# Four raw weight buffers and four for high halves, where there were five and three

## The reference, cut to what matters

```python
mod_l = silu(c) @ w_ada + b_ada                 # 6 x 2048 modulation values, and the same from c_ctx
h_l = modulate(rms_norm(x, g), sh_a, sc_a)      # and h_c from ctx
qa, kva, kr, cb, cc, ch = split(h_l @ w_in)     # latent attention (8 heads) and a gated convolution
x = x + gt_a * (mix @ w_out)
x = x + gt_f * (conv_glu(hf @ w_up) @ w_down)   # inner width 5504
x = rms_norm(x, g_final)
# block two, layer A: index scores, top-k, attention of 16 heads, gate, w_o, layer norm, gated embedding
# block two, layer B: stick-breaking attention of 16 heads, gate, w_o, layer norm, gated embedding
```

## Time and profile before

| what | us |
|---|---|
| median of 3 runs (lowest, highest) | 2374.26 (2372.83, 2378.23) |
| the profiled execution: its time | 2373.12 |
| the profiled execution: span from first to last instruction | 2371.4 |
| TensorE, VectorE, ScalarE busy | 2285.2, 1564.9, 1074.3 |
| granted TensorE clock, mean | 0.984 |

### The profile page before, as it was taken

One profiled execution on the slowest core, in us unless ns is written; L12 is line 12 of the kernel. 1 busy time (PEld: TensorE's weight loads), 2 busy tenths in 40 slices (PEclk: granted clock), 3 DMA queues, 4 the chain that ended last, 5 costly groups with the idle time before them and its releaser, 6 DMA issues.

```text
span 2371.4 us, 39488 instructions
## 1 busy us (share of the span) xinstructions
PE 2285.2 (96%) x17584; PEld 2165.7 (91%) x17584; DVE 1564.9 (66%) x1750; ACT 1074.3 (45%) x1014; POOL 42.0 (2%) x80
## 2 busy tenths in 40 slices
PE   6889999998999999999999899999999999999998
PEld 3568878898999999999999899989999999999998
DVE  6777797899868455554556768765567635445674
ACT  6564444334444334443444444445435436664352
POOL 0000000000000000000000000000000000000000
PEclk8999999999999999999999999999999999999999
DMA  8674785696766554455445444333544554335543
GB/s 349 257 275 178 284 302 231 249 350 228 292 249 225 185 189 182 179 185 188 178 181 198 156 179 159 142 120 136 189 160 167 189 179 159 114 135 178 178 160 125
DMA packets 64953, 471.85 MB, mean 199 GB/s; under 512 B 7216, under 2 KB 7216, under 8 KB 8336
## 3 DMA queue, kind: packets, MB, share of 16 engines
q1 hardware_dynamic: 55152, 399.21, 46.4%
q0 software_dynamic: 9488, 68.03, 7.6%
q10 hardware_dynamic: 144, 2.10, 0.2%
HBM read 467.21 MB, written 2.10 MB: 198 GB/s over the span
## 4 chain that ended last, share of the span: by engine, by line
PE 81%; DVE 12%; ACT 3%; issue 2%; DMA 1%; SPq 0%; DVEq 0%; ACTq 0%
PE acc L1898 73%; PE aux L1898 8%; DVE lo L971 4%; ACT hi L404 2%; DVE ada_acc L991 2%; DMA x<-x_t 1%; DVE x L1751 0%; DMA raw<-stream 0%; DVE x L1748 0%; DMA ctx<-ctx_t 0%; DVE rstd L1104 0%; DVE conv_sum L1282 0%; DVE act_lo L1758 0%; DVE rope_scratch L1597 0%; ACT probs L774 0%
## 5 line engine op out<-in xcount | busy, mean ns | idle before, releaser
L971 DVE TENSOR_TENSOR lo<-raw,hi 128x2048 fp32r<-128x2048 f32 x374 | 854.3, 2290 | 641.6 <-ACT hi L404 641.2
L404 ACT ACTIVATE hi<-raw 128x2048 fp32r<-128x2048 f32 x374 | 712.9, 1912 | 817.7 <-PE acc L1898 785.6
L1898 PE MATMUL acc<-act_hi,hi 128*128 128x256 f32 x4464 | 601.4, 288 | 15.1 <-ACT act_hi L730 5.8
L1898 PEld LDWEIGHTS acc<-act_hi,hi 128*128 128x128 f32 x4464 | 566.2, 194 | 30.2 <-issue 19.8
L1898 PE MATMUL acc<-act_lo,hi 128*128 128x256 f32 x4464 | 585.1, 284 | 0.0
L1898 PE MATMUL acc<-act_hi,lo 128*128 128x256 f32 x4464 | 581.2, 283 | 0.0
L1898 PEld LDWEIGHTS acc<-act_lo,hi 128*128 128x128 f32 x4464 | 559.9, 193 | 0.0
L1898 PEld LDWEIGHTS acc<-act_hi,lo 128*128 128x128 f32 x4464 | 555.8, 192 | 0.0
L991 DVE SCALAR_TENSOR_TENSOR ada_acc<-ada_raw,silu_c,ada_acc 128x512 f32<-128x512 f32 x224 | 152.9, 747 | 3.4 <-DMA ada_raw<-ada_stream 2.9
L1898 PE MATMUL acc<-u_hi,hi 128*128 128x256 f32 x688 | 89.8, 283 | 0.0
L1898 PE MATMUL acc<-u_lo,hi 128*128 128x256 f32 x688 | 89.7, 283 | 0.0
(11 more groups left out here) (328 smaller groups left out, 1647.7 us busy)
## 6 DMA issues: line engine op xcount, KB each, us to landing
raw<-stream SPq DMA_DIRECT2D x374, 1024.0 KB, 4.8
ada_raw<-ada_stream POOLq DMA_DIRECT2D x64, 1024.0 KB, 5.9
x<-x_t SPq DMA_DIRECT2D x1, 2048.0 KB, 15.6
ctx<-ctx_t SPq DMA_DIRECT2D x1, 2048.0 KB, 7.8
x<-x_t ACTq DMA_DIRECT2D x1, 2048.0 KB, 8.6
out<-x SPq DMA_DIRECT2D x3, 512.0 KB, 7.2
p_raw<-p_t POOLq DMA_DIRECT2D x1, 512.0 KB, 4.2
out<-x SPq DMA_DIRECT2D x2, 256.0 KB, 2.0
```

Of the source, the lines that this page charges most:

```text
L404: nc.scalar.activation(HI[c % NH][:, :], RAW[c % NR][:, :], ACT.Copy).then_inc(hi_done, 1)
L971: V.tensor_tensor(LO[c % NR][:, :], RAW[c % NR][:, :], HI[c % NH][:, :].bitcast(F32), ALU.subtract)\
L1898: return TE.matmul(out, lhs, rhs, start=start, stop=stop, skip_group_check=True)
```

## The change

Of eight buffers of 8 KB, four instead of five hold raw chunks (and low halves), and four instead of three hold high halves. The modulation groups of the opening lie in the same stream in both kernels. Nothing else changes: the instructions, their order and the addresses behind the eight buffers are the same, but the waits for `pe_chunk` in L349 and L403 have other values, and x % NR and x % NH go through four values.

```diff
-    NR, NH = 5, 3
+    NR, NH = 4, 4
```

## The result

Over 20 runs of each kernel the changed one has a median of 2376.91 us (2374.11 to 2382.78), the one before 2373.41 us (2370.86 to 2378.23): a ratio of 1.0015, 95% interval 1.0008 to 1.0021. The change costs 0.15%, which lies within the 0.2% that the prediction called no change, at its slower end. The profiled execution took 2377.09 us, with a span of 2375.4, 4.0 us longer than before.

A forecast was written before the change was run, and what follows sets the result against it. TensorE, busy 96%, was taken as the bound, with gaps in the opening and around norms and attentions. 2.9 + 3.0 - 0.7 - 0.6 - 1.8 - 1.2 - 2.0 + 1.4 = +1.0 us gave a 2375.3 us median, range 2369.5 to 2381.5.

The forecast's parts named there:

- The rule: Every high half: starts 4.8 us after the end of chunk c-4, not at c-3's end; gain is chunk time minus 4.8.
- Part 1: Opening, context load: issued at 36.45 instead of 33.53 because it waits for chunk 5; +2.9 us, bounds 2.0 to 4.5.
- Part 2: Opening bursts after w_in chunks: later loads, mainly load 38, delay the row copy; +3.0 us, bounds 1.9 to 5.0.
- half 42: High half at 187.6 us: waits for its load until 187.4; counted as a gain, -0.2 us.
- Part 3: Gains at several places after the opening, each the smallest of rule, VectorE's idle time and load limit: -0.7, -0.6, -1.8, -1.2, -2.0 us.
- Half 46: Around 217.45 us: this high half, ahead of the copy that frees a PSUM bank, comes earlier; -0.5 us.
- VectorE at 265 us: From 265 to 345 us VectorE is the bound; its 0.62 us wait for a half at the beginning goes; -0.6 us.
- the sums in w_out: Between 420 and 456 us: VectorE's 2.39 us wait for half 69 shrinks, limited by TensorE's scores; -1.8 us.
- Layer A: Block two, about 1465 to 1513 us: VectorE's waits shrink, limited by half 245 coming only 1.2 us earlier; -1.2 us.
- Part 4: Norm before the feed-forward part: half 86's load lands at 549.0 instead of a start at 547.6; +1.4 us, bounds 0 to 2.0.
- The slower rival: Landing over 5.76 us takes the gains except 0.7, parts 1, 2 and 4 stay: +6.6 us, 2381 us; chance 0.24.
- The faster one: Rival: parts 1 and 2 are absorbed and the fourth high buffer's gains come: -4.9 us, 2369 us; chance 0.08.

The follow-up runs named there:

- again44: The changed kernel (four raw, four high buffers) run once more with no edit, for a second profile: ratio 1.0014 to the kernel before, span 2376.8 us.
- The kernel before with both moves: Kernel before (five raw, three high), context load issued behind load 7 and GpSimd's second stream begun after chunk 35: ratio 0.9995, repeated with more rounds 0.9989.
- four variants of the changed kernel with a move: Changed kernel with context load ahead of buffer 9's wait (1.0011), ahead of load 8 (1.0002), GpSimd's stream after chunk 35 (1.0005), or the last two together (0.9989).
- before2: The kernel before run once more with no edit, for a second profile: ratio 1.0003, span 2369.8 us.

## Why the prediction was right, point by point

**The rule** (a high half starts one landing after the end of c-4) held; only its 4.8 us was too few at some places, as below. It shows in the 721 us of waits for loads and in the two layer norms: all six profiles with four and four buffers gain 0.9 to 1.1 us at each, and the one with four and three gains nothing. VectorE in the kernel after at the first of these:

```profile
1721.99 2.29 DVE L971 TENSOR_TENSOR lo<-raw,hi 128x2048 fp32r<-128x2048 f32 x1 [3.44 <-ACT hi L404]
1727.82 2.29 DVE L971 TENSOR_TENSOR lo<-raw,hi 128x2048 fp32r<-128x2048 f32 x1 [3.54 <-ACT hi L404]
1730.02 1.21 DVE L1779 SCALAR_TENSOR_TENSOR x<-x,acc 128x1024 f32<-128x1024 f32 x1
```

The low half ahead of the sums is at 1727.82, before at 1722.88: +4.94, where chunk 256 had ended at +5.92. Forecast -1.0 each, measured -0.94 each.

**Part 1** was mis-sized: +2.9 forecast, +4.1 and +4.0 measured from chunk 4 to chunk 9 in the two profiles of after, +4.2 by itself. I had let the context take its 7.79 us wherever it was issued. It took 8.9 to 9.2 us at the later place and 10.7 right behind load 8. The upper bound of 4.5 covered it. What it does after that, I had right: nothing takes it back.

**Part 2** came out at +3.3 (from 3.85 to 7.17 by chunk 42), and +5.6 in again44 (2.52 to 8.13), with 3.0 forecast and 1.9 to 5.0 as bounds; the second is outside them. Load 38 is as named: 158.1 issued, 10.0 us, 168.1 landed. The term of 0.2 for half 42 had the wrong sign. Its load is issued at 187.6:

```profile
L352 SPq DMA_DIRECT2D raw<-stream x1: 328/328/328, 187.6 to 187.6; - x1
...
  ACT hi L404: 4.2, 1
...
DMA to landing us min/median/max: 7.1/7.1/7.1
```

It lands at 194.7. Before, the half started at 187.6 behind other work of ScalarE, its load long landed; I had let the later load land just ahead of that. Chunk 40 had made up 2.45 us, and with this half 3.05 were lost again.

**Part 3, gains.** Half 46 (-0.5) and VectorE at 265 us (-0.6) gave nothing: the shift stays at +7.15 from chunk 44 to 70. At 265 us my own rule takes the gain away. Chunks 48 and 49 last 4.32 us each, and loads 51 and 52 took 5.1 and 5.6, so these two halves come later than the chunks do. VectorE before, then after, at the low half of chunk 52:

```profile
260.60 2.29 DVE L971 TENSOR_TENSOR lo<-raw,hi 128x2048 fp32r<-128x2048 f32 x1
```

```profile
268.47 2.29 DVE L971 TENSOR_TENSOR lo<-raw,hi 128x2048 fp32r<-128x2048 f32 x1
```

It starts 7.87 us later, with the chunks at +7.15, and the work behind it uses up the 0.62 us. I had checked the half at which VectorE stood idle and not the two ahead of it. Against the sums in w_out (-1.8) the shift falls by 3.3 (and by 2.5 in again44). VectorE in the kernel after, around the low half at which it had stood 2.39 us:

```profile
422.73 1.41 DVE L991 SCALAR_TENSOR_TENSOR ada_acc<-ada_raw,silu_c,ada_acc 128x512 f32<-128x512 f32 x2
424.06 2.28 DVE L971 TENSOR_TENSOR lo<-raw,hi 128x2048 fp32r<-128x2048 f32 x1
426.26 0.15 DVE L1262 RECIPROCAL columns<-columns 128x1 f32<-128x1 f32 x1
426.45 0.49 DVE L1263 TENSOR_SCALAR r<-r,columns 128x512 f32<-128x512 f32 x1
429.33 0.69 DVE L1256 TENSOR_REDUCE columns<-aux 128x1 f32<-128x512 f32 x1 [2.39 <-PE aux L1898]
```

The idle time ahead of the low half is gone, and the next maximum (L1256) now waits for TensorE's scores. It comes at 429.33, before at 423.74: +5.59, against +7.15 of the chunks, so 1.56 of the 1.8 us were there on VectorE, limited by the scores as forecast. By the low half of chunk 72 (454.81, before 448.70: +6.11) 1.0 of it was left. So at most 1 us of the 3.3 by which the shift falls can have come this way. Whether any of it reached TensorE isn't shown. With four raw and three high buffers the same low half waits as long as before and is as late as the chunks (428.06, before 420.94: +7.12):

```profile
428.06 2.29 DVE L972 TENSOR_TENSOR lo<-raw,hi 128x2048 fp32r<-128x2048 f32 x1 [2.39 <-ACT hi L405]
```

And still the shift falls by 3.9 us. The kernel before with both moves keeps this wait too, and its shift falls by 3.7. What all these kernels have in common is less time at the half clock. Windows of before, of after, of the kernel with GpSimd's stream later and of that with four raw and three high buffers, in this order:

```profile
440.00:500.00 60.00, 55.57 (x388) 50.23 (x388) 50.95 (x65) 19.60 (x16) 4.49 (x9) 0.89 0.75 289
```

```profile
440.00:500.00 60.00, 56.62 (x416) 52.09 (x415) 53.52 (x72) 19.50 (x17) 4.22 (x8) 0.94 0.77 292
```

```profile
440.00:500.00 60.00, 56.66 (x441) 52.69 (x441) 54.08 (x70) 21.31 (x18) 4.77 (x9) 1.00 0.79 306
```

```profile
440.00:500.00 60.00, 55.58 (x421) 50.50 (x420) 53.41 (x73) 21.39 (x18) 4.23 (x8) 0.97 0.77 297
```

Chunks 71 to 73 take 36.0 and 35.25 us in the two profiles of before, 32.7 and 33.6 in those of after, 29.6 in the third kernel, in which the window has no time at 1.2 GHz, and 32.1 in the fourth. So the fall in w_out is for the most part the clock's, and the forecast of -1.8 by the fourth high buffer isn't confirmed by it. How it divides between fewer gaps and the clock isn't settled: again44 and before2 both have 0.91 in this window, and again44 is still 1.7 us shorter.

Layer A (-1.2) gave +0.33 and 0. ScalarE in the kernel after:

```profile
1493.40 1.92 ACT L404 ACTIVATE hi<-raw 128x2048 fp32r<-128x2048 f32 x1 [3.89 <-DMA raw<-stream]
1495.22 1.01 ACT L549 ACTIVATE u<-acc 128x1024 f32<-128x1024 f32 x1
1500.54 1.91 ACT L404 ACTIVATE hi<-raw 128x2048 fp32r<-128x2048 f32 x1 [4.31 <-DMA raw<-stream]
```

The second is half 245. Its load took 6.2 us (6.0 in again44) where the sum had 4.8, and the low half behind it came at 1502.56, after 2.57 us of idle VectorE that hadn't been there at 1496.63. Where load 245 took 4.8 to 5.1 us, as in the four variants of the changed kernel with a move, layer A did give something: the shift falls by 1.2 us from chunk 240 to 256 in one of them and by 2.5 to 2.7 in the other three. These three had lost 1.5 us between chunks 86 and 240, for which the runs show no cause; from chunk 86 to 256 all four gain 1.0 to 1.3. With three high buffers layer A gives nothing. Why load 245 lands late in both profiles of after alone stays open. Here, in part 1 and at 265 us the step that failed is the landing time, taken as fixed at the median of the profile's page or at what the same load took before.

**A term that I had not seen:** +0.7 (and +0.4) at chunk 78. The load of chunk 77 took 10.7 and 10.5 us beside the second stream, and ended a lead of VectorE that I had called safe behind "some 7 to 9 us".

**Part 4** was +1.04 with +1.4 forecast. The load of chunk 86 took 7.2 us, within the 4.8 to 7.6 assumed.

**The sum.** +1.0 forecast, +4.0 in the profile, +3.5 in the medians. The misses: +0.95 in part 1 (1.2, less the 0.25 by which this profile began early), +0.5 from there to chunk 42, +1.1 for the two small gains, +0.7 at chunk 77, +1.5 in layer A and +0.1 at the norms; against them w_out's -1.5 and part 4's -0.35. Together +3.0, which is the profile's. The slower rival (loads take the gains wherever landing is as long as a chunk) was true in layer A (6.2 us against 5.76) and at 265 us (5.1 and 5.6 against 4.32), false at the layer norms, and untested in w_out, where the clock moved; the result lies between the forecast and it (+6.6). The faster one fell with the context's place on the chain. The stretch to 205 us was to be 4 to 8 us longer and is 7.2; the rest was to be 3 to 7 us shorter and is 3.1, just within. That is luck: 3.3 us of it fell in w_out with the clock, and in again44 the two are 8.1 and 2.65, both outside. The price in the opening, the cost at the norm and the small total were right, and the time lies in the range, but of the named gains only the 2 us of the layer norms are shown to come from the buffers in the changed kernel as it stands.

The forecast's estimate of 4.4 and 6.8 us for a load took 2.0 us plus the bytes by 436 GB/s for loads that SyncE issues. The Trainium skill (DMA: Bandwidth & Descriptors, section Anatomy of one DMA) states this fit for transfers that GpSimd issues. SyncE's took 4.8 and 7.8 us here, and no term of the sum used the formula.

## What to carry to other kernels

A buffer ring is two waits, one for the slot and one for the landing: moving a buffer from raw to derived data gains one chunk's time minus the landing time, so it is worth what the slowest landing in a stage leaves, not what the median leaves, and nothing where a chunk is shorter than a landing. Look at the loads that stand *behind* the ring's wait on the same engine without needing it: here one later wait ahead of one unrelated load cost 0.24% by itself (0.15 to 0.34), about as much as the whole change. And a stage that is full in the steady state says nothing about the ring's length: three raw buffers kept the feed-forward stages at 5.76 us a chunk and cost 9% elsewhere. Before a step of a trace is put down to a change, look whether it comes where the change is absent: the fall in w_out did.

## What the runs showed of the hardware

- **A load's landing depends on its neighbours in the queue.** The 2 MB context took 7.79 us with one load issued within 2 us behind it; 9.0 in after, with load 8 issued 2.9 us ahead and two loads within 2 us behind; 9.05 in the kernel before with the later wait, with three loads within 2 us behind and none still in flight ahead; 10.7 right behind load 8; and 14.9 among the early loads (19.41 to 34.32). The Trainium skill (DMA: Bandwidth & Descriptors, section Two DMAs through the same engine are not ordered) says that descriptors of one queue start in order but are pipelined. The 9.05 us agrees with it, if what starts later takes from what started first; no run here varies only the loads behind it.
- **A 1 MB load varies from 4.7 to 10.7 us beside the second stream**, and the same load does it in one profile after another (load 38: 9.4 to 10.6 in all eight profiles with four or five raw buffers and the other stream from chunk 32 on; load 77: 10.4 to 10.7 in four of the changed kernel's, about 5 in two), while starting the other stream three chunks later makes load 38 4.7 to 5.5. So load 38's time is contention with a place in the program, not chance; a trace of before shows it (9.4), if the landing is read for each load and not as a median. Load 77 has two levels in one kernel's variants, and what decides between them isn't shown.
- **The clock moves gains about.** The time at the half clock (1.2 GHz) was 79.3 and 72.5 us in two profiles of before, 67.5 and 84.3 in two of after. From chunk 70 to 73 the profiles with five and three buffers take 32.3 to 36.0 us and those with four and four 29.4 to 34.8, the shorter the less of it is at 1.2 GHz. So a step of 1 to 3 us beside an attention is near what one profile can show, and the experiments' totals over many runs decide, not a step of one trace.
